# Rotating all retention query and key chunks on GpSimd during attention, and storing them back to HBM

## The reference

```
h    = rmsnorm(x, g_pre) * (1 + scale) + shift
proj = h @ w_in            # c_q, c_kv, k_pe, gate_mla, q_ret, k_ret, v_ret, gate_ret, merges
y_mla = mla(c_q, c_kv, k_pe) * silu(gate_mla)            # 8 heads, causal, blocks of 128
q = rotary(q_ret); k = rotary(k_ret) * RET_QK ** -0.5     # 4 heads of 256
# per head and chunk of 128 tokens, with decays:
out = (q k^T * decay_in) v + xi * (q R);  R = gamma_c * R + (zeta * k)^T v
y_ret = groupnorm(out) * g_ret * silu(gate_ret)
x = x + gate * ((sigmoid(merge_mla) * (y_mla @ w_proj_mla) + sigmoid(merge_ret) * (y_ret @ w_proj_ret)) @ w_out)
return rmsnorm(x, g_final)
```

## Time and profile before

| What | Value |
|---|---|
| time, median of 3 runs (lowest, highest) | 1586.52 us (1585.24, 1587.58) |
| the profiled execution: its own time; its span | 1586.35 us; 1584.5 us |
| PE busy | 1540.6 us, 97% of the span |
| DVE, ACT, POOL busy | 994.8, 667.4, 415.9 us |
| mean granted clock of PE | 0.995 |

### The profile page before, as it was taken

How to read it: one execution, slowest core, us unless ns; L and a number is a source line. 1 busy time by engine, 2 the same in 40 slices (tenths; PEclk the granted TensorE clock), 3 DMA queues, 4 the chain that set the end, 5 groups by cost and what they waited for, 6 DMA issues and landing times. The chain is left out here.

```text
span 1584.5 us, 20414 instructions
## 1 busy us (share of the span) xinstructions
PE 1540.6 (97%) x7472; PEld 1287.2 (81%) x7472; DVE 994.8 (63%) x1629; ACT 667.4 (42%) x1144; POOL 415.9 (26%) x350
## 2 busy tenths in 40 slices
PE   5999999999999999999999999999899999999998
PEld 4788888888888888788888888887677888878886
DVE  6884444444444458752666665667988877799644
ACT  7553455543333353342343343434544444445311
POOL 0032233222322200200000000017778783522000
PEclk9999999999999999999999999999999999999999
DMA  9333232333323334699365554546988787889432
GB/s 381 104 136 113 107 113 107 114 108 118 120 106 107 94 108 156 260 413 339 134 207 176 173 200 172 186 140 229 307 268 265 255 271 240 297 286 309 156 107 80
DMA packets 154499, 299.55 MB, mean 189 GB/s; under 512 B 12048, under 2 KB 93072, under 8 KB 145696
## 3 DMA queue, kind: packets, MB, share of 16 engines
q1 hardware_dynamic: 137680, 265.80, 48.5%
q10 hardware_dynamic: 12080, 15.60, 2.9%
q0 software_dynamic: 4640, 16.84, 2.7%
HBM read 196.23 MB, written 100.93 MB: 188 GB/s over the span
## 5 line engine op out<-in xcount | busy, mean ns | idle before, releaser
L1894 DVE TENSOR_TENSOR w_form<-w_pair,w_form 128x512 fp32r<-128x512 f32 x150 | 116.3, 776 | 124.9 <-ACT w_form L1469 123.2
L1469 ACT ACTIVATE w_form<-w_pair 128x512 fp32r<-128x512 f32 x150 | 94.7, 632 | 216.8 <-PE p_banks L2433 211.7
L1551 ACT ACTIVATE prob<-p_banks,neg_max 128x128 f32<-128x128 f32 (+3 forms) x64 | 47.4, 741 | 183.1 <-DVE neg_max L2021 183.1
L1286 POOL DMA_DIRECT2D v_ret<-v_stage x32 | 17.5, 548 | 399.8 <-DVE v_stage L1998 399.5
L2430 PE MATMUL p_banks<-h_hi,w_form 128*128 128x512 f32 x300 | 116.7, 389 | 0.0
L2432 PE MATMUL p_banks<-h_lo,w_form 128*128 128x512 f32 x300 | 116.7, 389 | 0.0
L2433 PE MATMUL p_banks<-h_hi,w_form 128*128 128x512 f32 x300 | 116.7, 389 | 0.0
L1196 POOL TENSOR_TENSOR w_pair<-w_pair 128x512 f32<-128x512 f32 x25 | 32.5, 1299 | 235.4 <-DVE w_form L1894 235.4
L2712 PE MATMUL p_banks<-t_hi,w_hi 128*128 128x512 f32 x224 | 87.5, 390 | 2.2 <-DVE t_lo L1662 2.2
L2715 PE MATMUL p_banks<-t_hi,w_lo 128*128 128x512 f32 x224 | 87.2, 389 | 0.0
L2714 PE MATMUL p_banks<-t_lo,w_hi 128*128 128x512 f32 x224 | 87.2, 389 | 0.0
(11 more groups left out here) (348 smaller groups left out, 4482.7 us busy)
## 6 DMA issues: line engine op xcount, KB each, us to landing
w_pair<-in_w_pairs SPq DMA_DIRECT2D x25, 1024.0 KB, 4.8
v_ret<-v_stage POOLq DMA_DIRECT2D x32, 512.0 KB, 3.7
v_chunk<-v_ret SPq DMA_DIRECT2D x32, 512.0 KB, 3.9
w_raw<-in_w_ret SPq DMA_DIRECT2D x28, 512.0 KB, 5.5
w_raw<-in_w_dense SPq DMA_DIRECT2D x23, 512.0 KB, 5.8
act_t<-stage SPq DMA_DIRECT2D x40, 256.0 KB, 2.0
act_t<-stage_late SPq DMA_DIRECT2D x40, 256.0 KB, 2.0
ada<-in_w_ada SPq DMA_DIRECT2D x4, 2048.0 KB, 24.9
```

Source lines behind the costliest of these rows:

```text
L1469: self.nc.scalar.activation(self.form[f % FORM_SLOTS][:, 0, :], self.form_source(f), ACT.Copy).then_inc(self.form_hi, 1)
L1551: nc.scalar.activation(self.prob[:, g % 2, 0:width], p[:, 6:8, :].rearrange("p a n -> p (a n)")[:, 0:width], ACT.Exp, bias=self.neg_max[:, ...
L1894: nc.vector.tensor_tensor(self.form[f % FORM_SLOTS][:, 1, :], self.form_source(f), self.form[f % FORM_SLOTS][:, 0, :].bitcast(F32), ALU.su ...
```

## The change

`rotate_chunk` moves whole into attention. One chunk is rotated at each odd step g, chunk g // 2, after the stores of the units that are due there. The raw chunk and its tables are loaded to a place of their own, the result is written to another, and POOL stores it back over the raw chunk in `qk`; then POOL issues the loads of the next chunk. Since the loading place takes the 4 KB of staging place 1, all units but 1 and 31 share place 0. In the retention SP loads the rotated chunk (no tables), and ACT and PE wait for that load alone. The remaining lines rename semaphores that are now shared, and a wait on `v_up_stored` moves from ACT to POOL.

```
     def v_slot(self, unit):
-        return 2 if unit in (1, FILL_UNITS - 1) else unit % 2
+        return 2 if unit in (1, FILL_UNITS - 1) else 0
...
+        sp.wait_ge(self.rot_stored, 16 * (n + 1))
+        sp.dma_start(self.qk_raw[n % 3][:, :, :].rearrange("p c n -> p (c n)"), self.d["qk"][h, m])\
             .then_inc(self.chunk_loaded[n % 3], 16)
-        sp.dma_start(self.qk_raw[n % 3][:, 4:6, :], self.d["ret_tables"].rearrange("a p n -> p a n")[:, :, m * P:(m + 1) * P])\
-            .then_inc(self.chunk_loaded[n % 3], 16)
...
+        self.load_rotation(pool, 0)
         units = 0
         for g in range(STEPS + 4):
             while units < self.units_filled(g - 1):
                 self.store_fill(pool, units)
                 units += 1
-            if g == STEPS - 2:
-                for n in range(2):
-                    self.rotate_chunk(pool, n)
-        for n in range(2, CHUNK_STEPS):
-            if n == 9:
+            if g % 2 and g // 2 < CHUNK_STEPS:
+                self.rotate_chunk(pool, g // 2)
+        for k in range(1, CHUNK_STEPS, 2):
+            self.token_sums(pool, k)
+            if k == 3:
                 for unit in range(units, FILL_UNITS):
                     self.store_fill(pool, unit)
-            self.rotate_chunk(pool, n)
-            if n >= 4 and n % 2 == 0:
-                self.token_sums(pool, n - 3)
...
+    def load_rotation(self, pool, n):
+        h, m = divmod(n, NT)
+        pool.dma_start(self.rot_raw[:, :, :].rearrange("p c n -> p (c n)"), self.d["qk"][h, m]).then_inc(self.rot_loaded, 16)
+        pool.dma_start(self.rot_table[:, :, :], self.d["ret_tables"].rearrange("a p n -> p a n")[:, :, m * P:(m + 1) * P])\
+            .then_inc(self.rot_loaded, 16)
...
+        pool.wait_ge(self.rot_loaded, 32 * (n + 1))
         if n == 0:
             pool.wait_ge(self.v_stored[2], 16)
+        else:
+            pool.wait_ge(self.rot_stored, 16 * n)
+        self.nc.gpsimd.tensor_tensor(by_sine[:, :, :], raw[:, :, :], sin, ALU.mult).then_inc(self.qk_step, 1)
+        self.nc.gpsimd.tensor_tensor(raw[:, :, :], raw[:, :, :], cos, ALU.mult).then_inc(self.qk_step, 1)
         pool.wait_ge(self.qk_step, 4 * n + 2)
+        self.nc.gpsimd.tensor_tensor(by_sine[:, 2:4, :], raw[:, 0:2, :], by_sine[:, 2:4, :], ALU.subtract).then_inc(self.qk_step, 1)
+        self.nc.gpsimd.tensor_tensor(by_sine[:, 0:2, :], raw[:, 2:4, :], by_sine[:, 0:2, :], ALU.add).then_inc(self.qk_step, 1)
+        pool.wait_ge(self.qk_step, 4 * n + 4)
+        pool.dma_start(self.d["qk"][h, m], by_sine[:, :, :].rearrange("p c n -> p (c n)")).then_inc(self.rot_stored, 16)
+        if n + 1 < CHUNK_STEPS:
+            self.load_rotation(pool, n + 1)
...
     def high_qk(self, act, n):
-        act.wait_ge(self.qk_step, 4 * n + 4)
+        act.wait_ge(self.chunk_loaded[n % 3], 16 * (n // 3 + 1))
...
     def turn_keys(self, pe, n):
-        pe.wait_ge(self.qk_step, 4 * n + 4)
+        pe.wait_ge(self.chunk_loaded[n % 3], 16 * (n // 3 + 1))
```

More of the change, by code:

```diff
@@ L113 @@
 PAIR_CHUNKS = NT // 2
+SUMS_FROM, OUT_HI_FROM = 6, 11
 GROUPS_SPLIT = ((0, 1), (2,), (3,), ())
@@ L223, in __init__ @@
         self.y_full = z("y_full", 96, [P, 2, 256])
-        self.qk_raw = [z("qk_raw_%d" % n, kb, [P, 6, P]) for n, kb in enumerate((56, 59, 4))]
+        self.qk_raw = [z("qk_raw_%d" % n, kb, [P, 4, P]) for n, kb in enumerate((56, 59, 4))]
         self.qk = z("qk_chunk", 62, [P, 2, 8, P], F32R)
-        self.by_sine = [z("qk_by_sine_early", 98, [P, 4, P]), z("qk_by_sine", 0, [P, 4, P])]
+        self.rot_raw, self.rot_table = z("rotation_raw", 32, [P, 4, P]), z("rotation_table", 34, [P, 2, P])
+        self.by_sine = z("qk_by_sine", 98, [P, 4, P])
         self.v_chunk = [z("v_chunk_%d" % n, kb, [P, 2, RET_V], F32R) for n, kb in enumerate((52, 40, 48))]
@@ L327, in semaphores @@
         self.x_early = sem("x_t_early_ready")
-        self.x_late = sem("x_t_late_ready")
+        self.x_late = sem("x_t_late_ready_then_out_w_hi_ready")
         self.ada_part = sem("ada_part_summed")
@@ L438, in semaphores @@
         self.m_lo_ready = sem("m_lo_ready")
-        self.out_hi_ready = sem("out_w_hi_ready")
+        self.out_hi_ready = self.x_late
         self.out_lo_ready = sem("out_w_lo_ready")
@@ L1204, in gpsimd @@
                 nc.gpsimd.tensor_tensor(rot[:, 3, :], rot[:, 3, :], rot[:, 1, :], ALU.add).then_inc(self.rot_added, 1)
+        pool.wait_ge(self.v_up_stored[2], 16 * 4)
+        pool.wait_ge(self.tables_stored, 64 + 16)
+        for slot in range(4):
+            pool.wait_ge(self.stored[slot], 16 * PAIRS)
+        pool.wait_ge(self.raw_stored, 16 * RAW)
+        self.load_rotation(pool, 0)
         units = 0
@@ L1226, in token_sums @@
         nc = self.nc
-        before = 4 * (k // 2)
+        before = SUMS_FROM + 4 * (k // 2)
         even, odd = self.y_ret[(k - 1) % 4], self.y_ret[k % 4]
@@ L1265, in rotate_chunk @@
-        by_sine = self.by_sine[late]
-        cos, sin = (raw[:, c:c + 1, :].broadcast_to([P, 4, P]) for c in (4, 5))
-        pool.wait_ge(self.chunk_loaded[n % 3], 32 * (n // 3 + 1))
+        h, m = divmod(n, NT)
+        raw, by_sine = self.rot_raw, self.by_sine
+        cos, sin = (self.rot_table[:, c:c + 1, :].broadcast_to([P, 4, P]) for c in range(2))
+        pool.wait_ge(self.rot_loaded, 32 * (n + 1))
         if n == 0:
             pool.wait_ge(self.v_stored[2], 16)
-        elif n == 12:
-            for slot in range(3):
-                pool.wait_ge(self.v_stored[slot], 16 * sum(self.v_slot(unit) == slot for unit in range(FILL_UNITS)))
@@ L1582, in evict_fill @@
                 act.wait_ge(self.split_stored[slot], self.store_count[slot])
-        elif unit == 3:
-            act.wait_ge(self.v_up_stored[2], 16 * 4)
         if self.v_stores(unit):
@@ L2159, in vector_retention @@
             if n in (2, 3):
-                dve.wait_ge(self.v_stored[1], 16 * sum(self.v_slot(unit) == 1 for unit in range(FILL_UNITS)))
+                dve.wait_ge(self.qk_step, 4 * CHUNK_STEPS)
             elif n >= 4:
```

22 lines of the change are left out of this document (5 added, 17 removed).

## The result

The changed kernel takes 1632.9 us (median of 4 runs, 1631.7 to 1638.8) against 1586.2 for the kernel before in the same comparison (4 runs). The ratio is 1.030, with an interval of 1.027 to 1.033: 47 us slower, where I had forecast 6. The profiled execution has a span of 1629.9 us, 45.4 more than before.

A forecast was written before the change was run, and what follows sets the result against it. PE was taken as full in attention, DVE as behind early in the retention. Retention -9.0 and attention +14.3 us gave +5.3, a span of 1589.8 and a forecast of 1592 us, range 1580 to 1606.

The forecast's parts named there:

- What bounds the kernel: PE full in attention, where any wait reaching it is lost; DVE behind in the retention from 1090 to 1158 us.
- The retention, -9.0 us: Retention: shorter DVE instructions and one wait less give 8.1 us, plus 0.9 us at 1205 us; bounds 4 and 14.7.
- the wait for chunk 2: Retention: DVE's wait of 1.5 us for the rotation of chunk 2 goes.
- what it left to the token sums: Retention: token sums on POOL still meet `y_lo` or `w_lo` in steps 1, 3, 5 and 7, 1.6 us in all.
- One place, units 9 and 23: Attention: ACT waits 3.3 and 4.0 us for the preceding unit's store, costing +2.4 and +3.5 us.
- two dips: Attention: PE's clock falls after each stop of 2.4 us or more, 1.5 us added for each of units 9, 23, 7.
- unit 7: Attention: POOL is late with the store of unit 6, ACT waits 2.6 us, costing +2.4 us.
- For most units the store is issued some 10 us earlier and hidden. Four are close: Attention: with one staging place only units 9, 23, 7 and 29 wait for stores: +2.4, +3.5, +2.4, +0.5 us.
- the loaded cycle: Attention: POOL's rotation cycle takes about 11.6 us when SP's loads for the next head fill the DMA engines.
- calm cycle: Attention: POOL's rotation with its DMA issues and next load takes 8.5 us without SP's loads.
- Rival D: POOL bounds attention from a mean cycle of about 10 us, each 1 us above costing 32; 1608 at 10.5 us; chance 0.11.
- Operations in attention: Attention: rotations meet DVE's `w_lo` of v's weights, 0.5 to 1.1 us each, +1 us; the scalings are left out.
- rival E: Attention: DVE's scalings of the probabilities wait for POOL in about 16 steps, some 9 us, 1601; chance 0.03.

The follow-up runs named there:

- sp_and_tables: The changed kernel with SP issuing the units' stores and rotations going chunk by chunk over the heads, so tables load 8 times: 1581.0 us, ratio 0.997.
- no_rotations: The kernel before with the rotations left out altogether, the retention working on unrotated chunks: 1577.0 us, ratio 0.994.
- after: The changed kernel itself, against the kernel before: 1632.9 us, ratio 1.030.
- tables_once: The changed kernel with chunk 0 of all heads rotated first, then chunk 1, tables loaded for the first head only: 1619.2 us, ratio 1.020.
- one_place: The kernel before with one staging place for the units of values instead of two, rotations staying in the retention: 1596.6 us, ratio 1.006.
- stores_by_sp: The whole changed kernel, but SP instead of POOL issues the units' stores at the same steps: 1594.3 us, ratio 1.004.
- traffic_alone: The changed kernel without the four operations of each rotation, keeping loads, store and the one staging place: 1603.1 us, ratio 1.010.
- ops_alone: The kernel before without rotations, POOL doing four operations of their shapes per chunk in attention on a place never loaded or stored: 1582.0 us, ratio 0.997.

## Why the prediction was wrong

**What bounds the kernel: right.** PE is full in attention, and all that reached it was lost. In every version PE's idle time there is what the outputs came late by, with the clock's share.

**The retention, -9.0 us: right as a potential, not what the change got.** Without rotations and in `sp_and_tables` the spread falls by 9.0 us. The terms hold one by one. These are DVE's groups of `no_rotations` from 1082 to 1162 us:

```profile
L2179 DVE TENSOR_TENSOR y_lo<-y_raw,y_hi 128x1024 fp32r<-128x1024 f32 x8 | 10.1, 1285 | 0.0
L1594 DVE TENSOR_TENSOR qk_chunk<-qk_raw,qk_chunk 128x512 fp32r<-128x512 f32 x10 | 6.9, 692 | 0.0
L616 DVE TENSOR_TENSOR w_lo<-w_raw,w_hi 128x1024 fp32r<-128x1024 f32 x3 | 4.7, 1562 | 0.0
```

Against the earlier trace rows `y_lo` gives 4.8 us, eight `low_qk` 1.8, `w_lo` nothing and the wait for chunk 2 its 1.5, in all 8.1, which is the sum of the prediction after what it left to the token sums. That the whole agrees to a tenth is luck; PE's waits for `out_n` in these 80 us are still 3.4 us, where I had 2 or less. In the changed kernel the spread falls by 5.1 us. The kernels whose rotations are over in time have spreads of 236.3 to 237.4, those whose POOL is late at the handover (`after`, `tables_once`) 240.2 and 239.7. In the changed kernel that is seen in the first 20 us of the retention, with DVE busy 13.9 us and a clock of 0.91. The high part of unit 29 is written there at 1136.0 us, after an eleventh wait for a store, where the kernel before, moved by 51.3, would have it at 1134.2; that may be part of it. No run isolates these 4 us.

**One place, units 9 and 23: right to half a microsecond.** I had 3.3 and 4.0 us of ACT's wait, `one_place` shows 2.9 and 3.5. PE stopped for 2.0 and 1.1 + 1.9 us, and the clock fell after each. My sum of units 9 and 23 with two dips, 8.9 us, stands against 8.7; it has 5.9 us of waits and 3.0 of the clock, the trace 5.0 and 3.7, so part of the agreement is luck. This holds for the place alone. In the changed kernel ACT waits 4.0 us before unit 9, 4.7 before unit 7 (I had 2.6), and 9.2 before unit 23, whose store POOL issued 10 us late.

**The step that failed: "For most units the store is issued some 10 us earlier and hidden. Four are close".** It took the stores' times from the trace of before, and let POOL be late at a single one, unit 7. I noted that POOL would be "nearly full in attention and runs late against its stores wherever two rotations follow each other", but that sentence had no term in the sum beyond +2.4 for unit 7. Seven stores were issued late in attention, for 37.1 of ACT's 41.9 us of waits. With the stores on SP's queue attention's loss went from 51.3 to 6.4 us; 27 us of that are in none of the parts by themselves.

**What was mis-sized in it: the loaded cycle.** The calm cycle of 8.5 us was nearly right: 15 of 31 took 8.4 to 9.9. For a loaded one I had 11.6 us, and the other 16 took 11.2 to 18.1. POOL's own loads landed 3.5 and 3.6 us after issue in the median, but after up to 9.3 and 11.5 us while SP loads a head, and part of the long cycles is the ring: POOL waited 54 us for units that were not there yet. Each long cycle pushes those that follow, because a calm one leaves only 1 to 1.5 us to catch up.

**Rival D, at 0.11, was nearest, and had half of the mechanism.** It said that POOL's cycle bounds attention, with each microsecond above 10 worth 32; at 11.5 that is 48 us, and attention lost 51. It was right that the cycle reaches attention. But it does so only through the unit stores in the same queue: `stores_by_sp` has nearly the same cycle, 11.3, and loses 6.4 us in attention. Nor is POOL full in the changed kernel, with its 54 us of waits for units, and PE doesn't wait in every head, as I had written for D; it has no wait at all from 880 to 932 us.

**Two smaller terms.** Traffic was left out of the sum: beside POOL's added loads and stores the loads of `v_head` land later, which PE meets at once (9.7 us in `traffic_alone`, 2.3 in the changed kernel, where the other waits may cover it). Operations in attention I had at +1; they cost 4. I had left the scalings out on the strength of one row, and 63 of them were stretched by 6.0 us in all, six `w_lo` by 4.0. The Trainium skill (SBUF — State Buffer, Who interferes with whom) says that `tensor_scalar` can run in a 2-port mode, in which DVE and GpSimd lock each other out for a whole instruction, and the 33.0 and 39.0 us above agree. My rival E had the direction, at 0.03; how much of the 4 us comes by the scalings and how much by `w_lo` no run shows.

**The range.** It went up to 1606 because each uncertain cost was bounded by itself. No end of it held several late stores, though the ring (store behind rotation, ACT behind store, next unit behind ACT, rotation behind next unit) can be read from the description of the change.

## What to carry to other kernels

When work is moved to an engine that also issues transfers, first list what stands in its queue behind the new work and who waits for each. A queue with little slack passes every lateness on, and a single buffer turns that into a ring. Put short, urgent stores on a queue that comes to them in time, and ahead of the bulk loads: here that alone turned +47 us into +7, and with a shorter cycle on POOL (the tables loaded 8 times instead of 32) into -5, with the same operations and the same memory. And price a transfer that recurs 32 times by the distribution of landings in loaded and calm stretches, not by one row.

## What the runs showed of the hardware

- A store of 512 KB that was issued before a head's loads landed after 2.7 us, the same store 6 us behind them after 7.0. The two came from different queues, but the queue doesn't explain it: on POOL's a store with no such loads beside it landed in 2.9 us, and on SP's own queue in `stores_by_sp` the store at 1019.4 us, just ahead of a head's loads, took 3.0 us, and the one at 1026.1, 6 us behind them, 8.7.
- PE's clock fell after short waits. In the kernel before it is at 0.85 from 1100 to 1110 us, behind waits of 1.3 and 1.0 us; it is at 0.83 at 1140 to 1150 us in the changed kernel, where PE was idle for only 1.4 of the 10 us; and 0.83 at 1030 to 1040 us in `one_place`, behind waits of 1.1 and 1.9 us. In `ops_alone`, with three waits of at most 0.9 us, it stayed at 1.00, and so it did in the first 80 us of the retention of `no_rotations`, with five of at most 1.1 us. So the length of the longest wait alone doesn't tell.
- Rotations on POOL stretch the scalings (63 from 33.0 to 39.0 us) and `w_lo` (mean 1.22 to 1.89 us) on DVE, but not `pt_lo`, which reads PSUM and SBUF (96 in 50.2 us both in `no_rotations` and in `ops_alone`).
